# The first compression product of a sequence pair, spread over six page units of two sequences instead of the four page units of the even one

## The reference, cut to what matters

```python
def _compress(kv, pe, w1, b1, w2):
    B, lk, h, d = kv.shape
    n_cmp = (lk - CMP_BLOCK) // CMP_STRIDE + 1
    idx = jnp.arange(n_cmp)[:, None] * CMP_STRIDE + jnp.arange(CMP_BLOCK)[None, :]
    blk = kv[:, idx] + pe[:, None, :]
    blk = jnp.swapaxes(blk, 2, 3).reshape(B, n_cmp, h, CMP_BLOCK * d)
    return jax.nn.silu(blk @ w1 + b1) @ w2
...
    ck = _compress(kvh(fck, NSA_KV_HEADS), cmp_pe[0], cmp_w1[0], cmp_b1[0], cmp_w2[0])
    cv = _compress(kvh(fcv, NSA_KV_HEADS), cmp_pe[1], cmp_w1[1], cmp_b1[1], cmp_w2[1])
```

## Time and profile before

| | us |
|---|---|
| median of 3 runs (lowest, highest) | 1383.36 (1381.53, 1391.57) |
| the profiled execution, whole | 1392.23 |
| its span | 1390.2 |
| page phase and its end in layer 0, first transpose to the last product of L1204 | 434.27 to 570.79 |
| the same in layer 1 | 1120.53 to 1253.53 |
| granted TensorE clock, mean | 0.933 |

### The profile page before, as it was taken

One profiled execution on the slowest core, in us unless ns is written; L12 is line 12 of the kernel. 1 busy time (PEld: TensorE's weight loads), 2 busy tenths in 40 slices (PEclk: granted clock), 3 DMA queues, 4 the chain that ended last, 5 costly groups with the idle time before them and its releaser, 6 DMA issues.

```text
span 1390.2 us, 19116 instructions
## 1 busy us (share of the span) xinstructions
PE 1237.7 (89%) x6860; PEld 967.2 (70%) x6860; DVE 644.6 (46%) x1289; ACT 445.6 (32%) x882; POOL 188.8 (14%) x327
## 2 busy tenths in 40 slices
PE   6999797998996788899789998979889958889998
PEld 4887566876774555698678876678667635567987
DVE  2102445647336889613211134274672378993141
ACT  2134323256313555320011243132652145543100
POOL 0200030020005421400020001100200063204000
PEclk9999898999988989999999998989999878999999
DMA  6454075444228853636254532644613397428352
GB/s 160 141 116 137 31 227 148 114 133 122 81 72 255 247 150 107 174 132 151 94 126 123 129 99 79 232 116 121 173 53 92 105 289 221 141 65 242 105 148 84
DMA packets 244580, 192.43 MB, mean 138 GB/s; under 512 B 119830, under 2 KB 226358, under 8 KB 243206
## 3 DMA queue, kind: packets, MB, share of 16 engines
q1 hardware_dynamic: 229222, 140.02, 36.8%
q0 software_dynamic: 15264, 51.19, 11.3%
HBM read 178.74 MB, written 20.80 MB: 144 GB/s over the span
## 4 chain that ended last, share of the span: by engine, by line
PE 72%; DVE 11%; DVEq 5%; issue 4%; ACT 3%; SPq 2%; DMA 2%; ACTq 1%; POOLq 0%; POOL 0%
PE ps L792 18%; PE ps L926 12%; PE ps L1273 6%; PE ps L1291 4%; DVEq L1956 4%; PE ps L798 4%; PE ps L1144 3%; DVE top L1953 3%; PE ps L1174 2%; DVE work L1955 2%; PE ps L1248 2%; DVE arena L1971 2%; PE ps L949 2%; PE ps L1059 1%; DMA arena<-in_cache_kv_dram 1%
## 5 line engine op out<-in xcount | busy, mean ns | idle before, releaser
L1316 ACT ACTIVATE arena<-ps 64x256 f32<-64x256 f32 (+13 forms) x382 | 206.2, 557 | 422.2 <-PE ps L1174 116.3
L792 PE MATMUL ps<-hT,slab 128*128 128x264 f32 (+1 forms) x1248 | 301.7, 400 | 8.9 <-DVE hT L1674 6.4
L792 PEld LDWEIGHTS ps<-hT,slab 128*128 128x128 f32 (+1 forms) x1248 | 241.7, 196 | 58.3 <-issue 11.6
L926 PE MATMUL ps<-hT,slab 128*128 128x264 f32 x768 | 190.0, 406 | 0.0
L926 PEld LDWEIGHTS ps<-hT,slab 128*128 128x128 f32 x768 | 150.5, 200 | 35.7 <-issue 7.6
L1174 PE MATMUL ps<-cst,arena 128*128 128x128 f32 x512 | 83.2, 317 | 58.0 <-DVE arena L1971 33.4
L1174 PEld LDWEIGHTS ps<-cst,arena 128*128 128x128 f32 x512 | 69.5, 165 | 83.7 <-issue 61.3
L532 POOL DMA_DIRECT2D arena<-in_cache_kv_dram x64 | 34.6, 541 | 435.3 <-PE ps L895 271.3
L1971 DVE COPY arena<-ps 64x256 f32<-64x256 f32 x128 | 76.1, 594 | 21.1 <-PE ps L1174 15.5
L1273 PE MATMUL ps<-Y,slab 128*128 128x264 f32 x384 | 85.8, 386 | 0.0
L1273 PEld LDWEIGHTS ps<-Y,slab 128*128 128x128 f32 x384 | 73.0, 190 | 12.5
(11 more groups left out here) (356 smaller groups left out, 1548.9 us busy)
## 6 DMA issues: line engine op xcount, KB each, us to landing
slab<-in_w_in_dram SPq DMA_DIRECT2D x48, 1024.0 KB, 5.2
slab<-in_w_in_dram SPq DMA_DIRECT2D x82, 256.0 KB, 3.7
arena<-in_cache_kv_dram SPq DMA_DIRECT2D x64, 192.0 KB, 3.5
arena<-in_cache_kv_dram POOLq DMA_DIRECT2D x64, 192.0 KB, 3.9
arena<-in_cache_kv_dram SPq DMA_DIRECT2D x64, 128.0 KB, 4.8
arena<-in_cache_kv_dram POOLq DMA_DIRECT2D x64, 128.0 KB, 6.1
slab<-in_w_branch_dram SPq DMA_DIRECT2D x16, 512.0 KB, 5.7
slab<-in_w_out_dram SPq DMA_DIRECT2D x8, 1024.0 KB, 4.8
```

Source lines behind the costliest of these rows:

```text
L792: last = mm(ps[0:job[3], n % 2, 0:LT], v[:, k, job[2]:job[2] + job[3]], hT[:, k, :], start=(k == 0), stop=(k == KD - 1))
L926: last = mm(ps[:, bank, 0:LT], v[:, k, (d % 2) * 128:(d % 2) * 128 + 128], hT[:, k, :], start=(k == 0), stop=(k == KD - 1))
L1316: return A(out, in_, ACT.Copy, scale=scale)
```

## The change

The 16 products of a pair are cut at 3, 6, 9, 12 and 14 into six parts of 3, 3, 3, 3, 2 and 2. Part 0 stands in the even sequence's unit j = 3, parts 1 to 5 in the units j = 0 to 4 of the odd sequence after it. `shift` and `join` move to that odd sequence's j = 4, `hidden` to the next even sequence's j = 0, `compressed` to its j = 1 and `take_compressed` to its j = 2. For pair 2 there is no next even sequence: its `hidden`, `compressed` and `take_compressed` stand behind the loop, ahead of pair 3. The explicit waits for "h g" ahead of the copies into `cT` go; `shift` and `join` now stand ahead of those copies.

```diff
@@ -448,7 +448,7 @@
-        dc_a = Steps("dc_a", sum([[f"hb {g}", f"hid {g}", f"c {g}"] for g in GR[:-1]], []) + ["scores", "hb 3", "hid 3", "c 3"]
+        dc_a = Steps("dc_a", sum([[f"hb {g}", f"hid {g}", f"c {g}"] for g in GR[:-1]], []) [:-1] + ["scores", "c 2", "hb 3", "hid 3", "c 3"]
                      + ["e cmp", "t cmp", "e", "PT"])
@@ -1137,12 +1137,14 @@
+                PARTS = (0, 3, 6, 9, 12, 14, 2 * ST)
+
                 def compress(g, part):
 
-                    kv = part // 2
-                    for t in range(4 * (part % 2), 4 * (part % 2) + 4):
+                    for n in range(PARTS[part], PARTS[part + 1]):
+                        kv, t = n // ST, n % ST
                         last = mm(ps[:, 7, kv * 256:(kv + 1) * 256], w1[:, kv, t, :], cT[:, g % 2, kv, t, :], start=(t == 0), stop=(t == ST - 1))
-                    if part == 3:
+                    if part == len(PARTS) - 2:
                         last.then_inc(dc_p.sem, dc_p.mark(f"h {g}"))
@@ -1179,18 +1181,19 @@
                     if w:
                         page_scores(w - 1)
-                    if s % 2 == 0 and s >= 2 and j < 4:
-                        if j == 0:
-                            taken_from(w - 2)
-                            if s >= 4:
-                                pe.wait_ge(dc_a.sem, dc_a(l, f"c {s // 2 - 2}"))
-                        compress(s // 2 - 1, j)
-                    if s % 2 == 1 and s >= 3 and j == 1:
-                        compressed((s - 3) // 2)
+                    if s % 2 == 0 and s >= 2 and j == 3:
+                        if s >= 4:
+                            pe.wait_ge(dc_a.sem, dc_a(l, f"c {s // 2 - 2}"))
+                        compress(s // 2 - 1, 0)
+                    if s % 2 == 1 and s >= 3:
+                        compress((s - 3) // 2, j + 1)
+                    if s % 2 == 0 and s >= 4 and j == 1:
+                        compressed(s // 2 - 2)
                 page_scores(NW - 1)
                 taken_from(NW - 2)
+                compressed(2)
                 pe.wait_ge(dc_a.sem, dc_a(l, "c 2"))
-                for part in range(4):
+                for part in range(6):
                     compress(3, part)
@@ -1571,21 +1574,21 @@
                     if j < 4:
-                        if s % 2 == 0 and s >= 4 and j == 0:
-                            act.wait_ge(dc_p.sem, dc_p(l, f"h {s // 2 - 2}"))
                         for u in range(2):
                             last = copy(blocks_of(s, j, u)[:, :, 1], pairs_of(4 + 2 * (w % 2), 1, u))
                         last.then_inc(pg_a.sem, pg_a.mark(f"C {w}"))
-                    if s % 2 == 0 and s >= 2 and j == 3:
-                        shift(s // 2 - 1)
-                    if s % 2 == 0 and s >= 2 and j == 4:
-                        hidden(s // 2 - 1)
-                    if s % 2 == 1 and s >= 3 and j == 2:
-                        take_compressed((s - 3) // 2)
+                    if s % 2 == 1 and s >= 3 and j == 4:
+                        shift((s - 3) // 2)
+                    if s % 2 == 0 and s >= 4 and j == 0:
+                        hidden(s // 2 - 2)
+                    if s % 2 == 0 and s >= 4 and j == 2:
+                        take_compressed(s // 2 - 2)
+                hidden(2)
                 act.wait_ge(pg_p.sem, pg_p(l, f"s {NW - 1}"))
                 copy(SS[:, 0:PAST].rearrange("p (b c) -> p b c", b=2), ps[:, 0:2, :], SCALE)
                 copy(SW[0:ROWS, 0:WIN], ps[0:ROWS, 2, :], SCALE)
                 act.drain().then_inc(dc_a.sem, dc_a.mark("scores"))
+                take_compressed(2)
                 shift(3)
                 take(6)
                 hidden(3)
@@ -1964,14 +1967,12 @@
                     if j < 4:
-                        if s % 2 == 0 and s >= 4 and j == 0:
-                            ve.wait_ge(dc_p.sem, dc_p(l, f"h {s // 2 - 2}"))
                         ve.wait_ge(pg_p.sem, pg_p(l, f"T {w}"))
                         for u in range(2):
                             last = TC(blocks_of(s, j, u)[:, :, 0], pairs_of(4 + 2 * (w % 2), 0, u))
                         last.then_inc(pg_v.sem, pg_v.mark(f"C {w}"))
-                    if s % 2 == 0 and s >= 2 and j == 3:
-                        join(s // 2 - 1)
+                    if s % 2 == 1 and s >= 3 and j == 4:
+                        join((s - 3) // 2)
                     for _ in range(1 if j in (0, 2) else 2):
                         left_out(half)
                         half += 1
```

## The result

The changed kernel takes 1397.76 us (median of 13 runs, 1394.95 to 1399.44). The kernel before, on the same chip, takes 1389.10 us (median of 13 runs, 1381.53 to 1393.66). The ratio is 1.0066, with an interval of 1.0051 to 1.0082. That is +9.2 us on 1389.1 (7.1 to 11.4): the change makes the kernel slower. I had put +7.1 us, in a range of 1382 to 1398, and called that no more than a measurement can tell. Thirteen runs tell it.

A forecast was written before the change was run, and what follows sets the result against it. The prediction took VectorE to bound the page phase, with TensorE's even sequences stalling some pairs. Loop -9.1 and end +16.2 gave +7.1 us on a median of 1383.36: 1390.5 us, range 1382 to 1398.

The forecast's parts named there:

- the slow first products: Pair 3's 16 products behind the loop: a low clock at their start adds 0.75 us a layer.
- Step 1: Page loop: work moves into both sequences' slack, every pair runs at VectorE's pace; -6.3 and -2.8, together -9.1 us.
- Step 2: End of the page phase: pair 2's chain delays pair 3's 16 products; +8.1 us a layer, +16.2 in both.
- My upper bound: End of the page phase: `compressed(2)` at half speed and products at half clock for 3 us more; +9.2 a layer.
- Step 3: Behind pair 3's products: TensorE runs almost without a gap for 60 us and more, so nothing hides the end's cost.
- The bound of 1% on what a measurement can tell: Whole kernel: a measurement tells about 1% from no change; chance of a result within 1%: 0.85.
- the bounds at +3.9 and +9.3: Whole kernel: the forecast's own range, the end's 13.0 to 18.4 us less the loop's 9.1; 1387 to 1393 us.
- The first rival: Even sequences: the loop before loses more, all six pairs at 33.5 us; -1.6 us, 1381.8 us; chance 0.14.
- The second rival: Odd sequences, j = 0 to 4: the clock falls and eats the loop's gain; +13 to +22 us, near 1399; chance 0.15.

The follow-up runs named there:

- e6: Changed kernel with three of VectorE's search steps taken out per layer, in even sequences 2, 4 and 6: 1392.66 us, ratio 1.0024 to the kernel before.
- e7: Kernel before with three of VectorE's search steps taken out per layer, in even sequences 2, 4 and 6: 1386.97 us, ratio 0.9985.
- e2: Kernel before with only pair 2's steps moved to the end as in the change, products in their old places: 1408.48 us, ratio 1.0141.
- e5: Changed kernel with the projection `mix(6)` moved from behind L1207's products to ahead of `compressed(2)`: 1381.59 us, ratio 0.9945 to the kernel before.
- e3: Changed kernel with nine unused products in TensorE's gap ahead of `compressed(2)`: 1391.95 us, ratio 1.0025 to the kernel before.
- e4: Changed kernel with the last join one unit earlier, ahead of two of VectorE's search steps: 1390.83 us, ratio 1.0026 to the kernel before.
- e8: e1 with the join ahead of VectorE's copies in odd j = 2 and `compressed` in j = 4: 1382.28 us, ratio 0.9958 to the kernel before.
- e9: e8 with `hidden` moved to odd j = 3: 1383.31 us, ratio 0.9959 to the kernel before.
- e1: Kernel before with products spread in four parts of four, pair 2's steps kept inside the loop, `compressed` at odd j = 3: 1389.69 us, ratio 1.0000.
- e10: Changed kernel with both the earlier last join of e4 and the moved projection of e5: 1383.32 us, ratio 0.9965 to the kernel before.

## Why the prediction missed, point by point

The direction of the sum was right, and so were the parts it was made of; two steps failed. The first is the last one of the prediction, which took +7.1 us for no change. The second is a term of the end, the slow first products, put at 0.75 us a layer where 1.9 and 1.7 were measured.

- **Step 1, the loop: right, a little less than said.** By the same copies of j = 3 it gave 5.9 + 2.4 = 8.3 us, against 9.1. VectorE's joins had no wait over 0.43 us, "h" was marked in time in every odd sequence, and e6 and e7 show which engine bounds. The intervals forecast (30.6, 31.3 and 31.3 us) held within 0.4.
- **Step 2, the end: right in mechanism, too small in one term.** The gap was 4.28 and 4.64 us (I said 4.3), `compressed(2)` took 2.2 (2.4), the products began 7.28 and 7.64 us after the last copy (7.35). But I gave the slow first products 0.75 us, after the row at the start of s = 2, and they cost 9.07 - 7.17 = 1.9 in layer 0 and 1.7 in layer 1. The row was the wrong neighbour: there the transposes and scores ahead of the products ran for 3.8 us of the slow stretch; here only 2.2 us of small products stood ahead. My upper bound (+9.2 a layer) is what happened. This is the term that failed: +8.1 was +9.1 and +9.3, together 2.2 us too little.
- **Step 3, nobody hides it: right.** e2 gives +19.6 us for the end alone. The chain behind it is unchanged; but e5 shows that there was cover to be had, a projection that began 14 us after `compressed(2)`, and I had named none.
- **The bound of 1% on what a measurement can tell: wrong.** It was read off three runs that spread over 10 us. The median of 13 against 13 has an interval of 0.15% to either side, and 0.66% lies well outside it. With the sum at +7.1 and the bounds at +3.9 and +9.3, all of the forecast's own range was on the slow side, and the text should have said "slower".
- **The time itself: partly luck.** The forecast of 1390.5 us stood on a median of three runs, 1383.36; over 13 runs the kernel before takes 1389.10. So 5.7 us of the 7.3 between forecast and result come from the base. 1397.76 lies inside the range of 1382 to 1398 by 0.24 us only, in a part of it that was put there for a rival that did not come.
- **The chances.** The first rival (no slower, the loop before loses more) may be partly true: of the joins inside the loop, four of six waited in the profiled execution of before, all four in e2 and all six in e7. What the spreading saves may thus vary from execution to execution; before spreads over 12.1 us in 13 runs, the changed kernel over 4.5. The end outweighs it. The second rival (the clock falls in the odd sequences and eats the gain) did not come, though the clock did fall there: it was at 0.50 in the windows 476:478 and 506:508, early in s = 3 and s = 5 of layer 0, and at 0.53 in 1164:1166 of layer 1. The slack held it, and the longest stall of VectorE was 0.43 us. The Trainium skill's rule that I had weighed against the change (TensorE: Matmul & The Clock Gate, "A second HAM failure mode: psum-queue depth-cycling") agrees with the trace so far as the clock went on falling and rising in the loop, but it cost the loop nothing to speak of; the intervals agree with VectorE's pace within 0.4 us.

How the 9 us of the end divide, from e3 and e4: about 2.7 us are the clock (e3, layer 0) and some 2.6 the two search steps ahead of the join (e4: the products began 3.43 us earlier, of which 0.8 is `compressed` at full clock). The rest, 3.8 us, is the chain from the join through ScalarE and `compressed`. The Trainium skill (TensorE: Matmul & The Clock Gate, "What's actually happening") says that the ramp of the clock is under 1% of a typical kernel's span. This case agrees with the size, 1.9 + 1.7 us of products and about 1 us of `compressed` in each layer being 0.4% of 1397; but it is more than half of what the change lost.

**The sign of the change hangs on where pair 2's last steps lie.** Inside the loop, with `compressed` late enough that its input is nearly ready (e8, e9), the spreading is worth 0.4%; inside but one unit too early (e1), nothing. Behind the loop it costs 0.7%, unless TensorE is given other work there (e5, 0.9945, the fastest version run; its interval overlaps those of e8, e9 and e10).

e6's loops gave 8.3 us more than the changed kernel's in the traces, its runs 5.8. The projection behind L1207's products can account for that: it took 5.48 and 5.52 us in e6 and 3.83 twice in the changed kernel, 3.3 us in all.

What stays open: why e10 is not faster than e5. From the first transposes to the end of L1208's products its trace is ahead by 0.9 and 2.9 us in the two layers. Between the two phases, where the programs are the same, it takes 4.5 us longer; from 800 to 900 us its granted clock is 0.90 against 0.93, and from 1000 to 1105 us 0.92 against 0.95. No run shows why.

## What to carry to other kernels

When a stage is moved one iteration later to even out a loop, write down what the last iteration leaves behind the loop, and count its steps engine by engine: the gain is per iteration, the exposed chain is paid once for each pass of the loop, and it runs on an engine that has gone idle. Look first for work further down that needs nothing of that chain, and put it into the gap; it is worth its own time and the clock's. And before calling a sum too small to measure, ask what its sign is at both bounds.

## What the runs showed of the hardware

- **The clock also fell after short gaps, and like gaps did not decide it.** It fell after gaps of 1.63 and 0.79 us (e4, both layers), of 0.45 and 0.86 us (e3, layer 1) and of 1.20 and 0.36 us (e9, layer 1). It held after 0.44 and 0.86 us (e5, layer 0) and after 1.20 and 0.37 us (e9, layer 0). Each fall cost the 16 products about 1.7 us. These rows don't tell what decides it.
- **It also fell while TensorE was busy.** The projection right behind the page phase took 5.48 to 5.52 us, against 3.83, in both layers of e1, e2, e6 and e8 and in layer 0 of e7. In e1 the fall comes some 15 us after the wait of 3.57 us had ended:

```profile
563.00:565.00 2.00, 2.00 (x13) 0.81 (x12) 1.21 (x2) 0.59 (x1) 1.32 (x2) 1.00 0.28 76
565.00:567.00 2.00, 2.00 (x7) 1.51 (x7) 1.51 (x6) 0.00 (x0) 0.15 (x2) 0.81 1.04 279
567.00:569.00 2.00, 2.00 (x6) 1.48 (x5) 1.10 (x6) 0.00 (x0) 2.00 (x3) 0.50 0.86 227
```

TensorE is busy for all of these 6 us, and the clock goes from 1.00 to 0.50. L926's 16 records took 5.51 us there:

```profile
565.24 5.51 PE L926 MATMUL ps<-hT,slab 128*128 128x264 f32 x16
```

With it, DMA goes from a share of 0.28 to 1.04. The transfers alone do not do it: in the kernel before the share goes from 0.09 to 0.97 at the same place, in the changed one from 0.04 to 0.98, and the clock stays at 1.00. Whether the small products just ahead or the earlier gap have to do with it wasn't tried.
- **Work without use can pay.** Nine unused products, 4.15 us of TensorE in each layer, made the changed kernel 0.4% faster (e3).
